# Drains in place of VectorE's own waits, and a GpSimd memset beside every second gather

## The reference, cut to what matters

```python
def peer(xn, w_q, keys1, keys2, u, v):
    q = (xt @ w_q).reshape(T, PEER_HEADS, 2, PEER_HALF)      # 8 heads
    s1 = einsum('thd,nd->thn', q[:, :, 0], keys1)            # 128 keys
    s2 = einsum('thd,nd->thn', q[:, :, 1], keys2)
    v1, i1 = top_k(s1, 16);  v2, i2 = top_k(s2, 16)
    cand = (v1[..., :, None] + v2[..., None, :]).reshape(T, 8, 256)
    sc, ci = top_k(cand, 16)
    experts = i1[ci // 16] * 128 + i2[ci % 16]               # 8 x 16 = 128 a token
    gates = softmax(sc)
    hb = gelu(einsum('tkd,td->tk', u[experts], xn))
    return einsum('tk,tkd->td', gates * hb, v[experts])
```

## Time and profile before

| | |
|---|---|
| median of 3 runs | 3734.14 us (3730.91 to 3735.75) |
| profiled execution, span from first to last instruction | 3876.1 us |
| profiled execution's own time beside its span | none is given; the page has the span alone |
| PE / DVE / ACT / POOL busy, share of the span | 82% / 65% / 32% / 27% |
| gathers in the trace | 1024, first 2208.3 us, last 3858.1 us |
| mean granted TensorE clock | 0.915 of full |
| HBM read | 937.45 MB |

### The profile page before, as it was taken

How to read it: one execution, slowest core, us unless ns; L and a number is a source line. 1 busy time by engine, 2 the same in 40 slices (tenths; PEclk the granted TensorE clock), 3 DMA queues, 4 the chain that set the end, 5 groups by cost and what they waited for, 6 DMA issues and landing times.

```text
span 3876.1 us, 41778 instructions
## 1 busy us (share of the span) xinstructions
PE 3197.7 (82%) x15104; PEld 2320.4 (60%) x15104; DVE 2512.3 (65%) x4584; ACT 1236.1 (32%) x1913; POOL 1038.0 (27%) x1133
## 2 busy tenths in 40 slices
PE   8999999999999999999999875655567985555456
PEld 7897888968887688888886652222224672222122
DVE  6655676666765667664664566767664566676675
ACT  5445444444442445444443221111111212111110
POOL 2000000000000000000000166666663046666666
PEclk9999999999999999999999987777778997777778
DMA  6634555535554456562563489999998288999998
GB/s 215 208 124 147 196 192 186 186 115 182 182 195 150 141 165 200 169 219 85 180 218 131 164 316 366 374 372 370 371 369 300 72 325 339 370 369 373 378 361 335
DMA packets 413641, 940.79 MB, mean 243 GB/s; under 512 B 24688, under 2 KB 209552, under 8 KB 413472
## 3 DMA queue, kind: packets, MB, share of 16 engines
q0 software_dynamic: 150800, 547.19, 37.2%
q1 hardware_dynamic: 260784, 389.57, 29.7%
q10 hardware_dynamic: 1888, 1.84, 0.1%
HBM read 937.45 MB, written 1.05 MB: 242 GB/s over the span
## 4 chain that ended last, share of the span: by engine, by line
PE 59%; DVE 21%; another core or an unknown queue 8%; issue 8%; POOL 3%; DMA 1%; ACT 1%; DVEq 0%; POOLq 0%; ACTq 0%; SPq 0%
PE pair L1007 16%; PE pair L1013 8%; DVE wide_ring L2593 6%; PE pair L776 5%; PE pair L777 5%; PE pair L778 5%; PE pair L849 4%; PE pair L870 4%; DVE pair L2633 3%; DVE arena L2593 2%; PE pair L1401 2%; POOL wide_ring L2778 2%; PE pair L857 2%; DVE deep_ring L2593 1%
## 5 line engine op out<-in xcount | busy, mean ns | idle before, releaser
L1441 PE MATMUL pair<-wide_ring,arena 128*128 128x512 f32 x912 | 472.0, 664 | 366.4 <-issue 232.4
L1842 DVE TENSOR_TENSOR wide_lo<-wide_ring,wide_hi 128x2048 fp32r<-128x2048 f32 x212 | 486.0, 2293 | 393.4 <-ACT wide_hi L1536 392.2
L2753 POOL TENSOR_TENSOR small<-small,minus_half 128x1 f32<-128x1 f32 (+2 forms) x31 | 25.1, 811 | 2302.3 <-DVE small L1999 1606.3
L1007 PE MATMUL pair<-x_both,wide_hi 128*128 128x512 f32 x2688 | 639.8, 390 | 0.0
L1441 PEld LDWEIGHTS pair<-wide_ring,arena 128*128 128x128 f32 x912 | 187.0, 212 | 637.7 <-issue 519.4
L1007 PEld LDWEIGHTS pair<-x_both,wide_hi 128*128 128x128 f32 x2688 | 498.5, 188 | 99.5
L1536 ACT ACTIVATE wide_hi<-wide_ring 128x2048 fp32r<-128x2048 f32 x212 | 404.4, 1912 | 456.2 <-DMA wide_ring<-in_ffn_w_gate_up 304.8
L2593 DVE CUSTOM_DVE_ANT_0 wide_ring<-wide_ring,pair 128x1024 f32<-128x1024 f32 x306 | 369.2, 1213 | 34.0 <-issue 25.1
L1013 PEld LDWEIGHTS pair<-x_both,wide_lo 128*128 128x128 f32 x2688 | 344.6, 191 | 13.1
L1013 PE MATMUL pair<-x_both,wide_lo 128*128 128x256 f32 x2688 | 348.7, 283 | 0.0
L2778 POOL DMA_INDIRECT wide_ring<-in_peer_v,pk_idx x318 | 307.4, 967 | 148.4 <-issue 93.2
(11 more groups left out here) (372 smaller groups left out, 5528.4 us busy)
## 6 DMA issues: line engine op xcount, KB each, us to landing
wide_ring<-in_ffn_w_gate_up SPq DMA_DIRECT2D x174, 1024.0 KB, 9.6
deep_ring<-in_ffn_w_down SPq DMA_DIRECT2D x88, 1024.0 KB, 5.0
wide_ring<-in_sb_w_qkv SPq DMA_DIRECT2D x12, 2048.0 KB, 12.6
wide_ring<-in_w_in SPq DMA_DIRECT2D x12, 2048.0 KB, 9.9
wide_ring<-in_moba_w_qkv SPq DMA_DIRECT2D x6, 2048.0 KB, 12.1
wide_ring<-in_peer_w_q SPq DMA_DIRECT2D x6, 2048.0 KB, 10.0
deep_ring<-in_sb_w_o SPq DMA_DIRECT2D x8, 1024.0 KB, 7.6
deep_ring<-in_w_out SPq DMA_DIRECT2D x8, 1024.0 KB, 7.5
```

Source lines behind the costliest of these rows:

```text
L1007: mm(work[2 * j + u][:, 0:2 * TOK], wide_hi[:, split_at(ph, j), k, u], x_both[:, k].rearrange("p a t -> p (a t)"), start=k == 0, stop=Fals ...
L1441: ins = mm(acc[t][h][:, :], pk_diag[:, s % 2, k], row_at(ph, row)[:, h * 512:(h + 1) * 512], start=first, stop=last, skip_group_check=True)
L1842: V.tensor_tensor(wide_lo[:, split_at(ph, j)], half_panel(ph, wide_ring[:, slot], j), wide_hi[:, split_at(ph, j)].bitcast(F32), ALU.subtra ...
```

## The change

VectorE in the expert layer: the wait for its own `pick_stage` ahead of each stage becomes a drain; only stages 7 and 14 still raise the semaphore (one for ScalarE's gates, one for GpSimd's gathers), and the two waits on it count accordingly. The reciprocal raises nothing, and the coefficients drain in place of the wait for it. The accumulate drains in place of the waits for `coef` and for the last `row_used`. GpSimd: after every second gather of a layer it waits until the memset of the pair before has been raised, and writes zeros to one column (128 partitions x 1) of a scratch tile that nobody reads, raising `paused`. The semaphore `paused` takes the place of `rden`.

```diff
+PICK_SIGNALS = (7, PICK_STAGES - 1)
+PICKED_GATES, PICKED_ROWS, PICK_RAISES = 1, 2, 2
...
+        pk_pause = sb("pk_pause", [P, 1])
...
 def gates(s):
-    act.wait_ge(S["pick_stage"], PICK_STAGES * (STEPS * i + s) + 8)
+    act.wait_ge(S["pick_stage"], PICK_RAISES * (STEPS * i + s) + PICKED_GATES)
...
 def pick_stage(ph, s, n):
                 if n == 0:
                     dve.wait_ge(S["key_scores_read"], UNITS * i + unit_of(h, t) + 1)
                 else:
-                    dve.wait_ge(S["pick_stage"], PICK_STAGES * (STEPS * i + s) + n)
+                    dve.drain()
...
-                ins.then_inc(S["pick_stage"], 1)
+                if n in PICK_SIGNALS:
+                    ins.then_inc(S["pick_stage"], 1)
...
                 def reciprocal(s):
                     dve.wait_ge(S["gate_exp"], STEPS * i + s + 1)
-                    V.reciprocal(pk_rden[:], pk_den[:, s % 4:s % 4 + 1]).then_inc(S["rden"], 1)
+                    V.reciprocal(pk_rden[:], pk_den[:, s % 4:s % 4 + 1])
                 def coefficients(s):
-                    dve.wait_ge(S["rden"], STEPS * i + s + 1)
+                    dve.drain()
                     dve.wait_ge(S["gelu"], STEPS * i + s + 1)
...
                 def accumulate(s, n):
-                    dve.wait_ge(S["coef"], STEPS * i + s + 1)
+                    dve.drain()
                     row = ROW_NUMBER["v", s, n]
                     await_row(dve, ph, row)
...
-                    rows = on_vector(s)
-                    before = ("v", s, rows[rows.index(n) - 1]) if n > 0 else ("v", s - 1, on_vector(s - 1)[-1])
-                    dve.wait_ge(S["row_used"], ROWS_USED * i + ROW_AFTER[before][1])
...
 def gather(ph):
                     if table == "u" and n == 0:
-                        pool.wait_ge(S["pick_stage"], PICK_STAGES * (STEPS * i + s + 1))
+                        pool.wait_ge(S["pick_stage"], PICK_RAISES * (STEPS * i + s) + PICKED_ROWS)
...
                     ).then_inc(row_in[slot], 16)
+                    if k % 2:
+                        pauses = len(ROWS) // 2 * i + k // 2
+                        if pauses > 0:
+                            pool.wait_ge(S["paused"], pauses)
+                        G.memset(pk_pause[:], 0.0).then_inc(S["paused"], 1)
```

More of the change, by code:

```diff
@@ L465, in build @@
             "gelu",
-            "rden",
+            "paused",
             "coef",
```

## The result

| | before | after |
|---|---|---|
| median of 20 runs each | 3733.78 us (3729.31 to 3737.84) | 3740.64 us (3732.16 to 3742.67) |
| traced execution, span | 3876.1 us | 3730.4 us |
| mean granted TensorE clock in it | 0.915 | 0.955 |
| after / before, timed | | 1.0014, 95% interval 1.0008 to 1.0020 |

The forecast was 3676 us. The change costs about 5 us by the ratio (the medians lie 6.9 us apart), 0.14%: inside what was called no change, and on the slower side. The traces say the opposite, 146 us less. Both are true: the traced execution of the kernel before was not like the ones that were timed.

The account below looks back on a forecast made before the run. It took a swing between full DMA rate and starvation, caused by late raises, as the bound. 62 us from pace less 2 us at the starts gave 60, scaled to 58: 3676 us, range 3600 to 3750.

Parts of the forecast that it names:

- what was called no change: Whole kernel: a timed difference within 0.2% (7 us), about what a measurement can tell; chance of same 0.23.
- The premise of the sum: Expert stages: pace now 1.409 us a gather, falling to 1.342 over 927 gathers, 62 us.
- the floor by the DMA engines: Expert-stage gathers: 512 KB at 411 GB/s takes 1.276 us a gather, the lowest pace transfers allow.
- VectorE's 0.24 us a gather of waiting for itself: Expert stages: VectorE loses 0.24 us a gather to its own late-arriving raises, which drains would take away.
- The median against the span: Whole kernel: median 142 us below the profiled span, read as profiling slowing it somewhere; gain scaled by 3734 / 3876.
- already at the rate: Rival, expert stages: late raises belong to the profiled execution, unprofiled pace 1.256 us a gather; 3734 us, chance 0.23.
- The argument from matmuls: TensorE's stages: profiling may stretch matmuls, 0.227 against 0.216 us each, an estimated 146 us outside the steady expert stretches.
- Price of a drain: VectorE in expert layers: 0.11 us each, 312 drains, 34 us a layer, beside the transfers.
- Exposed at the first picks: Picks of steps 0 and 1, ahead of the first gathers: drains cost 1 us a layer, 2 us for both.
- Memset and wait: GpSimd after every second gather: memset fits between gathers, taken as 0 us; its wait is free if raises are prompt.
- The brake: GpSimd's memset wait: holds gathers while raises are late, preventing starvation; rival that it binds, 3823 us, chance 0.15.
- The upper bound for a memset: GpSimd between gathers: 0.46 us if a memset takes as long as the power operation; 3793 us.

Follow-up runs that it names:

- e1: The kernel before, nothing edited, timed and traced again: 3734.46 us, ratio 1.0003.
- e3: The kernel before plus only the memsets and their waits, no drains: 3735.45 us, ratio 1.0001.
- e7: The kernel before plus the memsets and waits, each memset of 128 columns in place of 1, no drains: 3737.68 us, ratio 1.0012.
- e8: The kernel before with three 128-column memsets and their waits in place of one after every second gather, no drains: 4016.16 us, ratio 1.0755.
- e9: The kernel before with v rows gathered for 64 of the 128 tokens: 4030.06 us, ratio 1.0752.
- e11: The kernel before with v gathers at half width, 128 rows of 2 KB in place of 4 KB: 3704.86 us, ratio 0.9916.
- e4: The changed kernel with 16 scratch columns in turn, each memset waiting only for the one 16 pairs earlier: 3740.38 us, ratio 1.0017.
- e12: The changed kernel with v gathers at half width, rows of 2 KB in place of 4 KB: 3707.66 us, ratio 0.9924 to the kernel before.
- e2: The changed kernel without the memsets and their waits, so drains and fewer raises only: 3739.63 us, ratio 1.0016.
- e5: The changed kernel with own waits and all raises kept in the picks of steps 0 and 1: 3740.51 us, ratio 1.0015.
- e6: The changed kernel once more, unedited, for a second trace: 3739.98 us, ratio 1.0015.

## Why the prediction was wrong

- **The premise of the sum failed.** The prediction took 1.409 us a gather from the earlier trace rows as the pace of the kernel and (1.409 - 1.342) x 927 = 62 us as its gain. e1 shows 1.25, below the 1.276 that it had taken as the floor by the DMA engines: issue can run ahead of transfer by the length of the queue, and the stage is then set by the transfers, 268 MB / 409 GB/s = 655 us and 17 more at the two ends. There was nothing to gain but queue.
- **VectorE's 0.24 us a gather of waiting for itself** stands in that trace (0.22, as the 112.5 us are those of all 512 gathers), and in no other trace of any kernel. Whatever delayed those starts is a feature of one execution. That the drains would cure it, should such an execution come, wasn't tried: none of the later traces with own waits (e1, e3, e7, e8, e9, e11) has a "remote" in its waits.
- **The median against the span was seen and explained away.** The 142 us between them was the warning. "Profiling makes this kernel slower somewhere" scaled the gain by 3734 / 3876 in place of dropping it. The rival "already at the rate" placed all 142 us in the expert stages (measured 144.8), foresaw 1.256 us a gather (1.25) and 3734 us: it was right that the late raises belonged to the profiled execution, and wrong only if that means profiling as such, since e1 is a traced execution too.
- **The argument from matmuls fell.** Against that rival stood the 0.227 us matmul of the earlier trace rows, put down to stretching by the profiler. The Trainium skill, "TensorE: Matmul & The Clock Gate", section on the back-to-back issue gap, gives 0.216 us for it, as the gap of a single matmul, from which came an estimated 146 us of stretched TensorE. e1 has, in a span of 3732.7 us:

```profile
399.72 0.39 PE L777 MATMUL pair<-deep_lo,hid_hi 128*128 128x512 f32 x1
...
404.03 0.39 PE L778 MATMUL pair<-deep_hi,hid_lo 128*128 128x512 f32 x1
```

  Again 4.31 us over nineteen, 0.227 each, so the difference is no stretching. The 146 was also too high as worked out: it counts 13,659 matmuls as ones of 512 columns, and by the first trace's shapes some 5,540 of them are. That it came out like the 142 was chance.
- **Price of a drain.** Taken 0.11 us, measured 0.18 behind a dot and 0.04 between dependent operations, both against an own wait. Beside the transfers most of them are covered: VectorE's busy time in 560 us went from 429 to 446 us (operations that overlapped now follow one another) and its waits for u rows in the first layer from 80.4 + 30.4 + 17.6 = 128.4 to 88.3 us. Exposed at the first picks: 0.94 + 0.58 = 1.5 us of the 2 taken. The Trainium skill, "VectorE: DVE Perf Modes", section on the DRAIN you can't avoid, has own semaphores cost nothing. e1's rows agree (0.00 us behind a dot), and this was the rule to follow.
- **Memset and wait** were right in their price: 0 us, by e3, e4 and e12; the pair stays at 2.49 us. The brake that the sum also counted on doesn't exist. The upper bound for a memset holds a slip: 0.02 + 0.59 + 0.17 - 0.30 = 0.48 us, not 0.46.
- **The sign.** Drains give all of the +0.15% (e2, e3). Of some 5 us the first picks show 1.5, and the ten stages of the five traces with single drains (after, e2, e4, e5, e6) average 673.1 us against 671.7 for the four of e1 and e3: 2 x 1.4 = 2.8 us. That adds up to 4.3, but the stages of one kernel differ by up to 1.4 us between traces and the time outside them by 11, e7 without a drain has a stage of 674.0, and e5, which removes the first term, did not get faster. So it is shown that the drains cost it, and open where it lies.

Open too: what brings on an execution like the first trace. In it a gather took GpSimd 0.937 us and a dot VectorE 1.22 us, as elsewhere, and transfers ran at 411 GB/s between the stops. Counted from its semaphore records, it holds only 375 of 656 raises of `row_used` and 294 of 480 of `pick_stage` (e1: all). The same holds for semaphores that VectorE doesn't raise: each of the 26 landing semaphores `row_in` has 119 to 172 records, where e1 has 609 to 641. So raises of VectorE and of the gathers alike came late, came merged or are missing from the record. That "remote" idles meant VectorE's own late raises, and that drains would take them away, is thus an inference that no run here tests.

## What to carry to other kernels

Before a stage of the trace is costed, set its span against the timed runs: where they are 4% apart, find the stage that differs or take a second trace, and until then treat every stall in it as belonging to the difference, above all a wait of an engine for itself. Where a queue of transfers stands at its full rate, what makes the issuing engine quicker, or slower by no more than it is ahead of the transfers (2.57 us a pair in e7, not 3.09 in e8), only changes the length of the queue. A drain is not cheaper than an engine's wait for its own raise; in this kernel it was 0.04 to 0.18 us dearer. And a trace of its own can't place an effect of 5 us when two traces of the same kernel are 13 us apart.

## What the runs showed of the hardware

- Gathers of 128 rows of 4 KB are held at 409 GB/s, 163 ns of a DMA engine a row; at 128 rows of 4 KB and 2 KB in turn they ran at 315 GB/s with the engines 0.92 busy, where GpSimd's pace was the bound; with 128 and 64 rows of 4 KB in turn only 247 GB/s at 1.03 busy, 270 ns a row. Gathering fewer partitions was worse than gathering all.
- A gather of 64 rows takes GpSimd 0.90 us, of 128 rows 0.94: its price hardly depends on the rows.
- GpSimd has 0.30 us between two gathers in which a memset of 0.11 us fits whole; one of 0.22 us costs 0.08.
- One execution of an unchanged program showed VectorE idle for up to 4.84 us though the one raise it waited for came from an operation of its own that had long ended, again and again in both expert stages, which took 144.8 us more in all. Of 117 timed executions of it 116 were within 3729 to 3741 us and can't have had it.
- The granted clock falls to half for 3.4 us in some executions and not in others of the same kernel (near 335 us: 0.50 in e6, 1.00 in after).
